# Moving the activation buffers of a four-layer fp32 kernel to other addresses in SBUF, relative to the weight blocks

## The chip, the cores and the metric

One core of a Trainium2 chip. The metric is the device time of one execution in microseconds (us); lower is better. TensorE is called PE in the profile, and its weight loads PEld; DVE is VectorE, ACT is ScalarE, POOL is GpSimd, SP is SyncE.

## The reference, cut to what matters

The kernel computes two fp32 blocks one after the other for 512 tokens of width 1024: a layer with an RWKV-7 mixer, a layer with a convolution mixer (each followed by cross attention to 256 memory tokens and a feed-forward network of width 2816), then a layer with gated linear attention and softmax attention side by side and its own feed-forward network. Nearly all arithmetic is the dense products with weights:

```python
for layer in range(DEPTH):                       # 2
    h = rmsnorm(x, norm_mix_g[layer])
    out = rwkv7_time_mix(h, ...) or conformer_conv(h, ...)
    x = x + out
    x = x + memory_cross_attention(rmsnorm(x, norm_xattn_g[layer]), memn, w_q, w_kv, w_o)
    x = x + conv_ffn(rmsnorm(x, norm_ffn_g[layer]), ffn_w_in[layer], ffn_dw[layer], ffn_w_out[layer])
...
def conv_ffn(h, w_in, dw, w_out):
    u = causal_dwconv(h @ w_in, dw)
    gate, val = u[..., :D_FF], u[..., D_FF:]
    return (jax.nn.silu(gate) * val) @ w_out
```

## The kernel before, in words

Activations are held transposed: 128 partitions times (8 feature tiles, 512 tokens). The weights come from HBM as 388 units of 8 blocks; a block is 128x128 fp32, which is 512 bytes in each partition. SP loads a unit into one of four slots of `raw`, ACT copies it rounded to the format fp32r into `wh` (L1135), and POOL subtracts the two and writes the rest into `wl` (L489). Activations are split in the same way into a high and a low part: `acth` and `actl`, `hidh` and `hidl`, `headh` and `headl`, `memh` and `meml`, `mixh` and `mixl`, `yh` and `yl`. The helper `product` (L504) multiplies one block: three products (high by high, low by high, high by low), each in two halves of 256 tokens, so six matmuls of 256 columns, and each of them loads its weight block into PE by a weight load of its own. A dense stage is a loop over units: 48 matmuls for each output tile of 128 features (8 blocks), 132 for the second product of the feed-forward networks (22 blocks). The order on every engine is fixed by the program text and by semaphores; no scheduler moves anything.

The line in `product` that the text speaks of:

```python
for w, m, first, last in ((w_h, hi, start, False), (w_h, lo, False, False), (w_l, hi, False, stop)):
    for n in range(0, out.shape[1], HALF):
        ins = pe.matmul(out[:, n:n + HALF], w, m[:, n:n + HALF], ...)
```

SBUF is laid out by hand. `place` puts a buffer at the cursor, rounds its size up to 32 bytes and moves the cursor on; `at` puts one at a given address. The cursor starts at byte 2048 of each partition. First come the buffers that live all the time (`raw`, `wh`, `wl`, the residual stream `xt`, `acth`, `actl`, the parameters `par`, the constants `common`, the small vector `omu`, `tmp`, `sq`, `rstd`), then the zone (`zone` is its first byte), which every stage lays out anew: the buffers `mix*`, `head*`, `mem*`, `hid*` and `y*`, and those of the attention and scan stages, lie there. All steps within a buffer by which a matmul's operand is chosen in a dense stage (block, slot, feature tile, half of the tokens) are multiples of 512 bytes, so where an activation buffer lies relative to the weights modulo 512 is one number for each buffer, and every matmul of `product` from it has the same.

Worked out from the sizes: `wh` lies at 18432 and `wl` at 34816, both whole numbers of 512 from each other. `xt` has 8 x 513 columns, 16416 bytes, and ends at 67616, which is 32 bytes beyond a whole number of blocks from the weights. `acth` begins there and `actl` 16384 later. The zone begins at 115904, 192 bytes beyond a whole number.

Of the kernel before, what the change touches and what calls it, by code (L numbers as in the profile page):

```python
# [27 lines left out]
P = 128  # L28
D = 1024
KT = D // P  # L30
# [49 lines left out]
NPAR = _c  # L80
# [88 lines left out]
def build_program(nc, dram):  # L169
# [55 lines left out]
    with ctx:  # L225
        cursor = [2048]

        def size(shape):
            return 4 * int(np.prod(shape[1:]))

        def at(name, shape, dtype, offset):
            assert offset + size(shape) <= nc.sbuf_usable_end, (name, offset)
            return nc.alloc_sbuf_tensor_at(name, shape, dtype, offset=offset)

        def place(name, shape, dtype=F32):
            t = at(name, shape, dtype, cursor[0])
            cursor[0] += (size(shape) + 31) // 32 * 32
            return t
# [2 lines left out]
            return ctx.enter_context(nc.semaphore(name))  # L241


        raw = place("raw", [P, SLOTS, BLOCKS * P])
        wh = place("wh", [P, SLOTS, BLOCKS * P], F32R)
        wl = place("wl", [P, SLOTS, BLOCKS * P], F32R)
        xt_at = cursor[0]
        xt = place("xt", [P, KT, T + 1])
        act_at = cursor[0]
        acth = place("acth", [P, KT, T], F32R)  # L250
        actl = place("actl", [P, KT, T], F32R)
        par = place("par", [P, NPAR])
        common = place("common", [P, 3 * P])
        omu = place("omu", [P, 7 * KT])
        eps = place("eps", [P, 6])
        tmp_at = cursor[0]
        tmp = place("tmp", [P, 2, T])
        sq_at = cursor[0]
        sq = place("sq", [P, 2, T])
        rstd_at = cursor[0]  # L260
        rstd = place("rstd", [P, T])
        zone = cursor[0]
        ident, ones, blk64 = (common[:, j * P:(j + 1) * P] for j in range(3))
        b_eps, b_ln, b_gn, b_rn, b_q, b_eps2 = (eps[:, j:j + 1] for j in range(6))
# [40 lines left out]
        def both(name, shape, n):  # L305

            return [[core(f"{name}{g}{j}", shape) for j in range(n)] for g in range(2)]

        c_core = place("c_core", [P, 7, CH])
        m_n16, m_a, m_be, ident64 = c_core[:, 0, :], c_core[:, 1:4, :], c_core[:, 4:6, :], c_core[:, 6, :]  # L310
        ND, T1, CC = (both(n, [P, 4, CH], 2) for n in ("nd", "t1", "cc"))
        AN, BE, VB = (both(n, [P, m, 4, CH], 2) for n, m in (("an", 3), ("be", 2), ("vb", 2)))
# [2313 lines left out]
```

## Time and profile before

| | |
|---|---|
| median of 3 runs | 2825.18 us (2824.49, 2825.18, 2836.0) |
| the profiled execution | 2821.63 us |
| its span (first to last instruction) | 2819.8 us |
| PE busy | 2632.6 us, 93% of the span, 26234 matmuls |
| PE weight loads busy | 2470.4 us, 88% |
| DVE, ACT, POOL busy | 1451.2, 1158.7, 947.3 us |
| mean granted TensorE clock | 0.965 of full speed |

The profile comes from one execution, and its rows are read against that execution's own 2821.63 us. Matmuls overlap one another in the pipeline, so the mean duration of one (some 280 ns) is longer than the distance between the starts of two; the pace is read from a count in a stretch of time.

### The profile page before, as it was taken

The page shows a single profiled execution, that of the slowest core. Times are in us where ns is not written, and L with a number is a line of the kernel's source. Part 1 is how long each engine was busy: PE and PEld are TensorE (multiplying, and loading weights), DVE is VectorE, ACT ScalarE, POOL GpSimd, SP SyncE. Part 2 cuts the span into 40 slices and gives each one's busy share as a digit, 9 for nine tenths or more (in the row PEclk, how much of TensorE's full clock was granted, in tenths as well). Part 3 has the DMA queues.
Part 4 walks back from the last instruction along what each step waited for, and adds up shares of the span by engine and source line. Part 5 has one row for each costly group of instructions (what it writes and reads, how often), then busy time and mean ns, then how long its engine had stood idle before and what let it go on. Part 6 is the DMA issues. An engine that isn't in the chain of part 4 may idle for free.

```text
span 2819.8 us, 64649 instructions
## 1 busy us (share of the span) xinstructions
PE 2632.6 (93%) x26234; PEld 2470.4 (88%) x26234; DVE 1451.2 (51%) x2006; ACT 1158.7 (41%) x1666; POOL 947.3 (34%) x392
## 2 busy tenths in 40 slices
PE   4897899888999999999899999999999889999997
PEld 4885899687799999978697999999998758999997
DVE  6567544341267775289653677743143234655521
ACT  6542333435354443332543444334246532544432
POOL 1332000025234444433441344444443202444442
PEclk6998899989999999999899999999999999999999
DMA  2221000114122223322321222233222101222231
GB/s 106 75 86 57 4 5 5 65 54 156 60 69 92 100 90 105 104 98 74 106 83 38 90 89 97 98 105 117 85 91 72 42 5 53 98 89 90 100 103 65
DMA packets 61126, 219.92 MB, mean 78 GB/s; under 512 B 6688, under 2 KB 7072, under 8 KB 60320
## 3 DMA queue, kind: packets, MB, share of 16 engines
q1 hardware_dynamic: 57536, 206.43, 21.6%
q10 hardware_dynamic: 3424, 11.01, 1.0%
q8 instruction: 137, 2.24, 0.3%
q14 instruction: 29, 0.24, 0.0%
HBM read 213.22 MB, written 4.19 MB: 77 GB/s over the span
## 4 chain that ended last, share of the span: by engine, by line
PE 66%; issue 21%; DVE 8%; ACT 3%; POOL 3%; DVEq 0%; POOLq 0%; ACTq 0%
PE psum L504 59%; DVE psum L2229 5%; POOL wl L489 3%; PE psum L870 1%; PE psum L827 1%; PE psum L1045 1%; PE psum L1044 1%; DVE tmp L1837 0%; ACT wh L1135 0%; DVE fox_max L2422 0%; PE psum L1067 0%; PE psum L858 0%; DVE fox_p L2447 0%; PE psum L1047 0%; PE psum L547 0%
## 5 line engine op out<-in xcount | busy, mean ns | idle before, releaser
L489 POOL TENSOR_TENSOR wl<-raw,wh 128x1024 fp32r<-128x1024 f32 x388 | 947.1, 2446 | 1839.9 <-ACT wh L1135 1838.7
L504 PE MATMUL psum<-acth,wh 128*128 128x256 f32 x3808 | 769.8, 284 | 34.9 <-DVE actl L1794 18.1
L504 PE MATMUL psum<-actl,wh 128*128 128x256 f32 x3808 | 759.1, 281 | 0.0
L504 PE MATMUL psum<-acth,wl 128*128 128x256 f32 x3808 | 758.8, 281 | 0.0
L504 PEld LDWEIGHTS psum<-acth,wh 128*128 128x128 f32 x3808 | 587.8, 190 | 55.2 <-issue 30.8
L1135 ACT ACTIVATE wh<-raw 128x1024 fp32r<-128x1024 f32 x388 | 407.2, 1056 | 527.9 <-PE psum L504 527.4
L504 PEld LDWEIGHTS psum<-actl,wh 128*128 128x128 f32 x3808 | 587.3, 190 | 0.0
L504 PEld LDWEIGHTS psum<-acth,wl 128*128 128x128 f32 x3808 | 586.9, 190 | 0.0
L2159 DVE TENSOR_TENSOR cu<-psum,rstd 128x512 f32<-128x512 f32 x132 | 91.0, 690 | 235.1 <-PE psum L504 220.4
L504 PE MATMUL psum<-hidl,wh 128*128 128x256 f32 x1056 | 205.6, 276 | 0.0
L504 PE MATMUL psum<-hidh,wl 128*128 128x256 f32 x1056 | 205.6, 276 | 0.0
L504 PE MATMUL psum<-hidh,wh 128*128 128x256 f32 x1056 | 205.5, 276 | 0.0
L1833 DVE TENSOR_TENSOR xt<-xt,delta 128x512 f32 x56 | 40.4, 721 | 245.3 <-ACT delta L1220 245.1
L504 PEld LDWEIGHTS psum<-hidl,wh 128*128 128x128 f32 x1056 | 159.0, 188 | 0.0
L504 PEld LDWEIGHTS psum<-hidh,wl 128*128 128x128 f32 x1056 | 158.9, 188 | 0.0
L504 PEld LDWEIGHTS psum<-hidh,wh 128*128 128x128 f32 x1056 | 158.9, 188 | 0.0
L2229 DVE SCALAR_TENSOR_TENSOR psum<-gp,par,psum 128x512 f32<-128x512 f32 x210 | 142.3, 751 | 1.6
L1837 DVE TENSOR_SCALAR tmp<-xt,par 128x512 f32 x48 | 124.3, 2590 | 12.0 <-DVE xt L1833 12.0
L1518 ACT ACTIVATE ffn_sg<-ffn_cg 128x512 f32<-128x512 f32 x66 | 41.8, 634 | 145.4 <-DVE ffn_cg L2182 112.9
L504 PE MATMUL psum<-memh,wh 128*128 128x256 f32 x256 | 74.7, 292 | 7.1 <-POOL wl L489 7.1
L2176 DVE SCALAR_TENSOR_TENSOR ffn_cg<-cu,par,ffn_cg 128x512 f32<-128x512 f32 x44 | 79.8, 1814 | 0.0
L504 PE MATMUL psum<-headh,wh 128*128 128x256 f32 x384 | 76.9, 282 | 0.0
(409 smaller groups left out, 3985.0 us busy)
## 6 DMA issues: line engine op xcount, KB each, us to landing
raw<-in_weights SPq DMA_DIRECT2D x388, 512.0 KB, 3.4
xt<-in_x SPq DMA_DIRECT2D x4, 512.0 KB, 5.6
xt<-in_x ACTq DMA_DIRECT2D x1, 2048.0 KB, 9.3
out_x<-xt ACTq DMA_DIRECT2D x4, 512.0 KB, 2.9
mem<-in_mem ACTq DMA_DIRECT2D x1, 1024.0 KB, 11.1
memn<-memh ACTq DMA_DIRECT2D x1, 1024.0 KB, 3.9
memn<-meml ACTq DMA_DIRECT2D x1, 1024.0 KB, 6.8
memh<-memn ACTq DMA_DIRECT2D x1, 1024.0 KB, 7.0
```

What stands on the lines that cost most here:

```text
L489: pool.tensor_tensor(wl[:, s, :], raw[:, s, :], wh[:, s, :].bitcast(F32), ALU.subtract).then_inc(split_done, 1)
L504: ins = pe.matmul(out[:, n:n + HALF], w, m[:, n:n + HALF], start=first and n == 0, stop=last and n + HALF >= out.shape[1])
L827: ins = pe.matmul(bank[4 + tt // 2][:, (tt % 2) * MEM:(tt % 2 + 1) * MEM], query[:, 2 * h + k, tt * P:(tt + 1) * P], keys[:, 2 * h + k, :] ...
L870: ins = pe.matmul(bank[t % 4][:, :], vtok[:, mt, (2 * h + dt) * P:(2 * h + dt + 1) * P], probt[:, h % 2, mt, :], start=(mt == 0), stop=(mt ...
L1044: pe.matmul(bank[b][:, o:o + n], fq[r, p, qt * P:n], fk[r, p, 0:n], start=True, stop=False)
L1135: act.activation(wh[:, s, :], raw[:, s, :], ACT.Identity).then_inc(split_hi, 1)
L1518: act.activation(sg[:, s, :], cg[:, s, :], ACT.Silu if l < 2 else ACT.Gelu_apprx_tanh).then_inc(gate_ready, 1)
L1833: dve.tensor_tensor(xk, xk, buf[:, s, :], add).then_inc(x_ready, 1)
L1837: dve.tensor_scalar(t_, xk, pc(gain[0], k + col), pc(gain[1], k) if n == 2 else None, mul, mul if n == 2 else ALU.bypass).then_inc(val_rea ...
L2159: dve.tensor_tensor(cu[:, s, 2:T + 2], bank_of(t0 + s), rstd[:, :], mul).then_inc(evacuated, 1)
L2176: chain.step(dve.scalar_tensor_tensor(out=to, in0=cu[:, s, 1:T + 1], scalar=pc("ffn_dw", col + 1), in1=to, op0=mul, op1=add))
L2229: ins = dve.scalar_tensor_tensor(out=acc, in0=gp[:, k, j:j + T], scalar=pc("conv_dw", k * CONVW + j), in1=acc, op0=mul, op1=add)
```

## The change

A helper moves the cursor on to the next address that lies a given number of bytes beyond a whole number of 512 from the weights. It is called with 0 ahead of `acth` and with 64 ahead of the zone. `par`, `common` and `eps` now stand ahead of `acth`, and the vector `omu` (one minus the mixing factors, 224 bytes, used in the first mixer) is put into the first stage's zone, at its end.

```diff
+        def beside_weights(apart):
+            cursor[0] += (weights_at + apart - cursor[0]) % 512
+
         raw = place("raw", [P, SLOTS, BLOCKS * P])
+        weights_at = cursor[0]
         wh = place("wh", [P, SLOTS, BLOCKS * P], F32R)
         wl = place("wl", [P, SLOTS, BLOCKS * P], F32R)
         xt_at = cursor[0]
         xt = place("xt", [P, KT, T + 1])
+        par = place("par", [P, NPAR])
+        common = place("common", [P, 3 * P])
+        eps = place("eps", [P, 6])
+        beside_weights(0)
         act_at = cursor[0]
         acth = place("acth", [P, KT, T], F32R)
         actl = place("actl", [P, KT, T], F32R)
-        par = place("par", [P, NPAR])
-        common = place("common", [P, 3 * P])
-        omu = place("omu", [P, 7 * KT])
-        eps = place("eps", [P, 6])
         tmp_at = cursor[0]
         tmp = place("tmp", [P, 2, T])
         sq_at = cursor[0]
         sq = place("sq", [P, 2, T])
         rstd_at = cursor[0]
         rstd = place("rstd", [P, T])
+        beside_weights(64)
         zone = cursor[0]
...
         c_core = place("c_core", [P, 7, CH])
+        omu = place("omu", [P, 7 * KT])
```

Worked out from the sizes, the addresses and what they leave modulo 512 from the weights:

```
buffer                                     before            after
wh, wl, raw, xt                            0                 0
acth, actl                                 67616, 84000: 32  72704, 89088: 0
tmp, sq, rstd (midh, midl lie in sq)       192               0
zone: mix, head, mem, hid, y, gmid, ...    115904: 192       115776: 64
par / common                               32 / 448          32 / 448
```

No instruction is added, taken away or moved: on each of the five engines the list of instructions with their operands and shapes reads the same before and after, and only line numbers and addresses differ.

## Rows read from the trace of the kernel before

**Rows 1.** The page's first parts: busy time, and the span in 40 slices.

```profile
PE 2632.6 (93%) x26234; PEld 2470.4 (88%) x26234; DVE 1451.2 (51%) x2006; ACT 1158.7 (41%) x1666; POOL 947.3 (34%) x392
PE   4897899888999999999899999999999889999997
...
PEclk6998899989999999999899999999999999999999
```

**Rows 2.** The page's chain that ended last, by engine and by line.

```profile
PE 66%; issue 21%; DVE 8%; ACT 3%; POOL 3%; DVEq 0%; POOLq 0%; ACTq 0%
PE psum L504 59%; DVE psum L2229 5%; POOL wl L489 3%; PE psum L870 1%; PE psum L827 1%; PE psum L1045 1%; PE psum L1044 1%; DVE tmp L1837 0%; ACT wh L1135 0%; DVE fox_max L2422 0%; PE psum L1067 0%; PE psum L858 0%; DVE fox_p L2447 0%; PE psum L1047 0%; PE psum L547 0%
```

**Rows 3.** Groups by line and shape, PE: count, busy us, mean ns, idle before.

```profile
L504 PE MATMUL psum<-acth,wh 128*128 128x256 f32 x3808 | 769.8, 284 | 34.9 <-DVE actl L1794 18.1 <-DVE actl L1845 6.6 <-DVE actl L2299 5.5
...
L504 PE MATMUL psum<-hidh,wh 128*128 128x256 f32 x1056 | 205.5, 276 | 0.0
L504 PE MATMUL psum<-headh,wh 128*128 128x256 f32 x384 | 76.9, 282 | 0.0
...
L504 PE MATMUL psum<-memh,wh 128*128 128x256 f32 x256 | 74.7, 292 | 7.1 <-POOL wl L489 7.1
...
L504 PE MATMUL psum<-mixh,wh 128*128 128x256 f32 x176 | 40.2, 314 | 20.0 <-DVE mixl L1794 20.0
...
L504 PE MATMUL psum<-yh,wh 128*128 128x256 f32 x128 | 24.9, 276 | 0.0
```

**Rows 4.** Windows, PE: stretch, length, busy us (matmuls), granted clock, DMA.

```profile
880.00:1060.00 180.00, 180.00 (x1545) 1.00 0.28 94
1080.00:1190.00 110.00, 110.00 (x974) 1.00 0.31 106
```

**Rows 5.** The chain in order of time: start us, us, what; the PE pieces.

```profile
696.07 22.41 PE psum L504 x192
...
721.93 22.63 PE psum L504 x192
...
783.00 43.55 PE psum L504 x384
834.54 360.50 PE psum L504 x3120
1256.28 15.90 DVE psum L2229 x24
...
1459.04 22.61 PE psum L504 x192
1485.11 16.97 PE psum L504 x144
1540.64 43.55 PE psum L504 x384
1592.19 360.50 PE psum L504 x3120
1961.67 67.22 PE psum L504 x576
...
2442.39 360.52 PE psum L504 x3120
```

**Rows 6.** The timeline at 44 us, PE, granted clock at half: start, us.

```profile
44.20 0.63 PE L504 MATMUL psum<-mixh,wh 128*128 128x256 f32 x2
44.63 0.63 PE L504 MATMUL psum<-mixl,wh 128*128 128x256 f32 x2
```

**Rows 7.** The timeline from 2177.5 us, weight loads (PEld): start, us.

```profile
2177.56 0.98 PEld L992 LDWEIGHTS psum<-sct,gvt 128*128 128x128 f32 x8
2178.66 1.30 PEld L995 LDWEIGHTS psum<-gqk,gla_states 64*128 64x128 f32 x11
```

**Rows 8.** Windows, all engines, the convolution stage: busy us of each.

```profile
1195.00:1375.00 180.00, 164.28 (x1148) 140.06 (x1146) 164.32 (x241) 62.03 (x101) 69.88 (x29) 0.97 0.30 100
```

## The prediction

> **What bounds the kernel now.** I read the page first. PE is busy 93% of the span and its clock is granted in full in nearly all slices after the start [rows 1]; the chain that ended last is made of PE for 66%, and 59% of the span is the one line of `product` [rows 2]. "issue" in that chain is mostly the scan of small matmuls and the start, which the change does not touch. So the pace at which PE starts the matmuls of `product` sets most of the time, and the next question is whether this pace depends on where an operand lies. The groups by line and shape answer it in part: the mean durations differ by operand, 284 ns for `acth` and 276 for `hidh` and `yh`, though shape and weights are alike [rows 3]. Durations are not paces, so I take counts in windows. From 880 to 1060 us PE does nothing but the first product of a feed-forward network, from `acth` and `actl`: 1545 matmuls touch the 180 us, and as each lasts 0.28 us the pace is (180 + 0.28) / 1545 = 116.7 ns. From 1080 to 1190 us it is the second product, from `hidh` and `hidl`: (110 + 0.28) / 974 = 113.2 ns. The clock is 1.00 in both [rows 4]. The chain confirms it: 834.54 us begins a piece of 360.50 us with 3120 matmuls, which are 2064 from `act` (43 tiles of 48) and 1056 from `hid`; 2064 x 116.7 = 240.9, and what is left gives 119.6 / 1056 = 113.3 ns [rows 5]. It does not come from other engines: windows with POOL, ACT and DMA working in the same way show both paces, and each buffer keeps its own for over a thousand matmuls.
>
> Shorter pieces of the chain show the rest [rows 5]. Buffer `act`: 22.41 / 192 = 116.7, 67.22 / 576 = 116.7, but 22.63 / 192 = 117.9. Zone buffer `head`: 43.55 / 384 = 113.4 twice, but 22.61 / 192 and 16.97 / 144 = 117.8. So the buffers 32 bytes beyond a whole number of blocks run at 116.7 or 117.9, those 192 beyond at 113.3 or, rarely, at 117.8; a stream keeps the pace with which it set out.
>
> **How far down the pace could go.** 256 columns at 2.4 GHz are 106.7 ns; 113.3 and 116.7 are 6.6 and 10.0 above. At the half clock there is nothing above: two matmuls in 0.43 us, 215 ns each as the rounded starts give it, against 256 / 1.2 GHz = 213.3 [rows 6]. The loss exists only where both streams of PE (moving columns, weights) read at full speed, which fits reads that meet in SBUF. The weight loads have a floor of their own: in L995 each has only 64 columns to wait for, and the loads still start (1.30 - 0.19) / 10 = 111 ns apart; in L992 (0.98 - 0.19) / 7 = 113, of which the first distance is the longest [rows 7]. I take 111.7 as the floor of a load of 128 columns, since `product` has one load for each matmul. The changed pace lies between that and something above 117.9.
>
> **The change part by part.** No instruction is added, removed or moved, so all that can change is a duration.
>
> `acth`, `actl` from 32 to 0. Three groups of 3808, 11424 matmuls [rows 3]. Bounds from the rows: 111.7 below, and above 117.9 plus what closeness may add (below). I take 113.3, the pace of the buffers that lie an even number of 64 bytes from the weights, because the difference between 113.3 and 116.7 is 3.4 ns, which is 8 columns or 32 bytes of the moving stream at full clock: just what a start 32 bytes off a 64-byte line would add, and 0 has none of that. Certain to count are the 3 x 2064 = 6192 of the three long pieces, where the chain is PE alone [rows 5]: 6192 x 3.4 = 21.1 us. Of the other 5232, 768 stand in the convolution stage, where DVE is busy 164.3 of 180 us and the chain goes through its taps (15.90 us of L2229) [rows 5, 8]: they count nothing. The remaining 4464 run at 116.7 or 117.9, half and half, so 4.0 ns each, 17.9 us; some stand beside waits of PE on DVE and ACT (34.9 us before `acth`) [rows 3] or at the half clock, and I count 80%: 14.3 us.
>
> The zone from 192 to 64. 3 x (1056 + 384 + 256 + 176 + 128) = 6000 matmuls [rows 3], at 113.3 nearly all. 64 is again a whole number of 64-byte lines, so by the same reading nothing changes, except that the 336 matmuls of `head` at 117.8 may fall to 113.4: 336 x 4.4 = 1.5 us. Bounds: 111.7 gives 1.6 x 6000 x 0.9 = 8.7 us more, 116.7 (the pace of 32, the nearest value seen) costs 3.4 x 6000 x 0.9 = 18 us.
>
> `tmp`, `sq`, `rstd`, `par`, `common`, `omu`. DVE, ACT and POOL read and write them, and no row ties a duration of theirs to an address. `omu` is used only in the first mixer. Nothing, and if it were something, it would be hidden behind PE at 93%.
>
> What keeps pace: ACT and POOL have to split a unit per tile, 48 x 113.3 = 5.4 us, and POOL needs 2.4 us for one (947.3 us for 388); DMA is at 0.28. None becomes the bound; DVE between the tiles of a long piece does not either, since PE waits for it 0.0 us before `hidh` [rows 1, 3, 4].
>
> Sum: 21.1 + 14.3 + 1.5 = 37 us off the profiled execution's 2821.6, 2785. The median of the runs stands 3.6 us above the profiled one, so 2788.
>
> By the Trainium skill, "SBUF — State Buffer", section on who interferes with whom, the two read ports of PE are independent and PE never waits on anyone. If so, addresses could not matter and the sum would be 0; the rows show 113.3 against 116.7 at the same clock and shape, so on this point the trace does not agree. Its page "TensorE: Matmul & The Clock Gate", section on the back-to-back gap, gives N / 2.4 + 2.5 ns, 109.2 for 256 columns. No row of `product` gets there; by it the estimate would be some 95 us less, about 2730, and I give it no more than 0.03, within the second case below.
>
> **The rivals.**
>
> Both buffers at the floor of the loads, 111.7. For: a start at the same line lets the two streams meet where the load pauses between blocks; the fp32 products L992, whose operands `sct` and `gvt` lie a whole number of 512 apart, show loads at the same distance as L995 [rows 7]. Against: no buffer of `product` shows it now. Price: 6192 x 5.0 + 4464 x 5.6 x 0.8 + 8.7 + 1.5 = 61 us; 2764.
>
> `act` gains, the zone loses. 64 is nearer to 32 than to 192. Then -35 + 18 = -17; 2809.
>
> Nothing. The pace is set by how a stream starts, not by the address: `head` is seen at 113.4 and at 117.8 at one address [rows 5], and the sums of both kinds stay as they are. Against: no `act` piece is below 116.7 and all three long `hid` pieces are at 113.3. 2825.
>
> Slower. What costs is closeness: when the moving stream and the weights begin in the same part of SBUF, they meet at once and stay together. 192 costs 6.6 and 32 costs 10.0 ns, 0.7 more for 32 bytes less; continued, 0 gives 117.4 and 64 gives 116.0: 0.7 x 10000 + 2.7 x 5400 = +22 us, 2847. L992 speaks against it, but its 128 columns fill 112 ns, so that stream reads half as fast and can yield. It decides as soon as the zone goes above 113.3 by more than `act` comes down: at a zone of 116.7 (+18 us) `act` would have to gain less than 1.8 ns on its 10000.
>
> **How the numbers follow.** `act` at 113.3 with the zone as it is: 0.38. Both near the floor, or between: 0.24. `act` gains and the zone loses: 0.12. Nothing: 0.10. Slower: 0.16. The likeliest gives 2788. About 0.5%, 14 us, is what a measurement of this kernel can tell from no change. Faster by more holds the first two cases and most of the third, 0.72; within it 0.11; slower 0.17. The range runs from 2757, a little below the floor case, to 2832, which leaves out the slower case and little else.
>
> **What would show it.** In the profile after: the window of the first product of a feed-forward network with (180 + 0.28) / 0.1133 = 1591 matmuls in 180 us instead of 1545, each of the three long pieces at 3120 x 0.1133 = 353.5 us instead of 360.5, the mean of `acth` near 276 as `hidh` has now, and `hidh` unchanged. At 1614 in 180 us, or 348.5 us, it is the floor of the loads. 1545 or fewer is the end of this reading; so is a `hid` pace above 113.3, which would say that 64 is worse than 192. The prediction is wrong if the 117.8 pace, whose start I cannot read from any row, becomes the usual one at the new addresses, or if other waits of PE take up the time that the long pieces give back.

## The result, and the profile after

The change made the kernel slower: 2869.52 us median of 4 runs (2860.37 to 2879.96) against 2824.84 us of 4 (2822.17 to 2836.0), a ratio of 1.0152 with a 95% interval of 1.0106 to 1.0198. The prediction was 2788 us, in a range of 2757 to 2832, and gave slower 0.17. The profile comes from the shortest of the four executions.

The page of the changed kernel (lines are 7 further down: `product` is L511) answers to [rows 1, 2]:

```profile
span 2858.6 us, 64649 instructions
...
PE 2672.1 (93%) x26234; PEld 2516.0 (88%) x26234; DVE 1435.0 (50%) x2006; ACT 1157.6 (40%) x1666; POOL 945.9 (33%) x392
...
PE psum L511 64%; PE psum L648 8%; DVE psum L2236 5%; PE psum L834 1%; PE psum L877 1%; PE psum L1052 1%; PE psum L1051 1%; POOL wl L496 1%; PE psum L576 1%; DVE tmp L1844 0%; ACT wh L1142 0%; DVE fox_max L2429 0%; DMA c_post<-in_c_post 0%; PE psum L1074 0%; DVE prep_pt L1955 0%
```

PE is busy 39.5 us longer (2672.1 against 2632.6), DVE, ACT and POOL are not, and the span is 38.8 us longer. That points to PE's own pace. The shares of the chain do not say it: L648, the small matmuls of the scan, has 8% here and did not show before, and "issue" fell from 21% to 6%, though the stretch that holds the scan (from the end of `mix` to the next products of `act`) took 433.8 us against 431.8; the chain was followed through it another way. Two windows of the changed kernel answer to [rows 4]; the second begins 10 us later, since the second product itself begins 9 us later:

```profile
880.00:1060.00 180.00, 180.00 (x1502) 1.00 0.26 90
1090.00:1200.00 110.00, 110.00 (x936) 1.00 0.30 103
```

With the last digits as in the prediction: (180 + 0.28) / 1502 = 120.0 ns for `acth` and `actl` at distance 0 (bytes beyond a whole number of 512 from the weights), where 32 had 116.7; (110 + 0.28) / 936 = 117.8 ns for `hidh` and `hidl` at 64, where 192 had 113.2. The clock is 1.00 in both, as before. The chain in order of time has the same pieces as [rows 5], each longer:

```profile
698.70 23.04 PE psum L511 x192
...
725.19 23.04 PE psum L511 x192
...
783.43 45.24 PE psum L511 x384
...
836.67 372.06 PE psum L511 x3120
...
1606.51 372.06 PE psum L511 x3120
1987.58 69.11 PE psum L511 x576
...
2469.96 372.06 PE psum L511 x3120
```

Every piece of `act` now gives one pace, 23.04 / 192 = 69.11 / 576 = 120.0, and `head` 45.24 / 384 = 117.8 where it had 113.4. The three long pieces are 372.06 - 360.50 = 11.56 us longer each, 34.7 of the 38.8 us in all.

### The profile page after: what moved, and what is told of

The parts are those of the page before. It is cut to its first block, busy times and chain, and to the rows that moved or that the text cites. A ratio compares the mean times of both kernels' runs of the same rounds, so it can differ in the third digit from the quotient of the medians.

```text
span 2858.6 us, 64649 instructions
## 1 busy us (share of the span) xinstructions
PE 2672.1 (93%) x26234; PEld 2516.0 (88%) x26234; DVE 1435.0 (50%) x2006; ACT 1157.6 (40%) x1666; POOL 945.9 (33%) x392
## 4 chain that ended last, share of the span: by engine, by line
PE 79%; DVE 10%; issue 6%; ACT 3%; POOL 1%; DMA 0%; DVEq 0%; ACTq 0%; POOLq 0%
PE psum L511 64%; PE psum L648 8%; DVE psum L2236 5%; PE psum L834 1%; PE psum L877 1%; PE psum L1052 1%; PE psum L1051 1%; POOL wl L496 1%; PE psum L576 1%; DVE tmp L1844 0%; ACT wh L1142 0%; DVE fox_max L2429 0%; DMA c_post<-in_c_post 0%; PE psum L1074 0%; DVE prep_pt L1955 0%
## 5 line engine op out<-in xcount | busy, mean ns | idle before, releaser
L511 PE MATMUL psum<-acth,wh 128*128 128x256 f32 x3808 | 781.9, 287 | 37.3 <-DVE actl L1801 21.1
L511 PE MATMUL psum<-actl,wh 128*128 128x256 f32 x3808 | 771.0, 284 | 0.0
L511 PE MATMUL psum<-acth,wl 128*128 128x256 f32 x3808 | 770.6, 284 | 0.0
L511 PEld LDWEIGHTS psum<-acth,wh 128*128 128x128 f32 x3808 | 598.7, 193 | 57.9 <-issue 30.6
L511 PEld LDWEIGHTS psum<-actl,wh 128*128 128x128 f32 x3808 | 598.1, 193 | 0.0
L511 PEld LDWEIGHTS psum<-acth,wl 128*128 128x128 f32 x3808 | 597.5, 193 | 0.0
L511 PE MATMUL psum<-hidl,wh 128*128 128x256 f32 x1056 | 210.3, 280 | 0.0
L511 PE MATMUL psum<-hidh,wh 128*128 128x256 f32 x1056 | 209.4, 280 | 0.0
L511 PE MATMUL psum<-hidh,wl 128*128 128x256 f32 x1056 | 209.3, 279 | 0.0
L511 PEld LDWEIGHTS psum<-hidh,wl 128*128 128x128 f32 x1056 | 161.3, 188 | 0.0
L511 PEld LDWEIGHTS psum<-hidh,wh 128*128 128x128 f32 x1056 | 161.2, 187 | 0.0
L511 PEld LDWEIGHTS psum<-hidl,wh 128*128 128x128 f32 x1056 | 161.2, 188 | 0.0
L511 PE MATMUL psum<-memh,wh 128*128 128x256 f32 x256 | 74.7, 292 | 7.2 <-ACT keys L1451 7.2
L511 PE MATMUL psum<-headh,wh 128*128 128x256 f32 x384 | 77.9, 283 | 0.0
```

The source lines that it names most:

```text
L511: ins = pe.matmul(out[:, n:n + HALF], w, m[:, n:n + HALF], start=first and n == 0, stop=last and n + HALF >= out.shape[1])
```

## The experiments

The question was what sets a pace. My reading had been the start on a 64-byte line; the result pointed to the distance of the two operands, but one number for each of two buffers, in one kernel, does not show that, and the second pace of `head` before was unexplained. Theory A is that the distance modulo some period decides; the rivals are the other engines, the start on a line, the place of the moving buffer by itself, and the stream that ran before.

### The pace by itself, for 16 distances (e1_pace)

```diff
+seen = [at(f"d{d:03d}x", [P, 4, T], F32R, 67584 + 18432 * (i % 2) + d) for i, d in enumerate(OFFSETS)]
...
+for k in range(8):
+    for j, s in enumerate((0, 0, 1)):
+        for h in range(0, T, HALF):
+            ins = pe.matmul(bank[w % 4][:, h:h + HALF], weights[:, s, k * P:(k + 1) * P],
+                            m[:, k % 4, h:h + HALF], ...)
```

> This kernel leaves the whole computation out except a stream of matmuls like product's, and copies x to the output. For each of 16 distances (0, 32, ... 480 bytes, modulo 512) between the moving buffer and the weights it runs six stretches of 48 fp32r matmuls of 256 columns, each stretch begun after a wait on VectorE of another length, and two stretches of 24 matmuls of 512 columns. No DMA runs, and ScalarE and VectorE do next to nothing. Theory A (the distance modulo 512 alone sets the pace, by the two read streams of TensorE meeting in SBUF): about 120.0 ns at 0, 116.7 at 32, 117.8 at 64, 113.3 at 192, as in the kernels before and after, with nothing else running. Theory B (reads and writes of the other engines make the loss): with them silent every distance goes at one pace, 109 to 113 ns. Theory C (what my prediction took: a start off a 64-byte line is what costs): the odd multiples of 32 are 3.4 ns slower than the even ones everywhere, which the 120 ns at 0 in the changed kernel already speaks against. For 512 columns with one load each the load is no limit: 213.3 ns plus at most 10, so at least 5 ns less for each 512 columns than two of 256.

The timeline of this kernel, PE: start us, us, and the idle time ahead. L243 is a stretch of 48 matmuls of 256 columns, L237 one of 24 with 512; the number in the name is the distance in bytes.

```profile
27.87 6.01 PE L243 MATMUL psum<-d000x,weights 128*128 128x256 f32 x48 [0.76 <-DVE step L219]
...
62.35 5.75 PE L237 MATMUL psum<-d000x,weights 128*128 128x512 f32 x24 [0.97 <-DVE step L219]
...
136.40 5.92 PE L243 MATMUL psum<-d064x,weights 128*128 128x256 f32 x48 [0.76 <-DVE step L219]
...
170.41 5.79 PE L237 MATMUL psum<-d064x,weights 128*128 128x512 f32 x24 [0.97 <-DVE step L219]
...
353.73 5.73 PE L243 MATMUL psum<-d192x,weights 128*128 128x256 f32 x48 [0.76 <-DVE step L219]
...
380.07 5.92 PE L243 MATMUL psum<-d192x,weights 128*128 128x256 f32 x48 [0.92 <-DVE step L219]
386.96 5.86 PE L237 MATMUL psum<-d192x,weights 128*128 128x512 f32 x24 [0.97 <-DVE step L219]
...
461.59 6.02 PE L243 MATMUL psum<-d256x,weights 128*128 128x256 f32 x48 [0.76 <-DVE step L219]
```

In such a stretch the first two starts are 0.22 us apart and the last matmul lasts 0.28 us, so 6.01 is (6.01 - 0.22 - 0.28) / 46 = 119.8 ns, 5.92 is 117.8, and 5.73 is 113.7, of which the first few starts are up to 124 ns apart and all later ones 113.3. From the starts of all stretches, once they are steady, in ns:

```
distance   0     32           64     96     128            160          192                 224
256 col.   120.0 116.7, 117.8 117.8  120.0  118.6          117.4, 118.7 113.3 x5, 117.8 x1  118.3
distance   256   288          320    352    384            416          448                 480
256 col.   120.0 116.7, 117.8 117.8  120.0  118.6, 120.0   117.4, 118.8 113.3 x5, 117.8 x1  118.3
512 col.: 226.7 at 0 and 256; 228.9 at 64 and 320; 233.2 to 234.5 at all others
```

Nothing else runs beside these stretches but, at most distances, four copies by ScalarE of 0.6 us each, and the paces of both kernels come back to the tenth of a ns: theory B is out. The period is 256 bytes, not 512, as far as steps of 32 bytes can tell. Theory C, mine, is out too: 0 and 96 are both the slowest, 64 and 128 are no better than 160. And for one distance there can be two paces; after its first few starts a stretch keeps to one of them.

### One part of the change at a time, and both buffers at 192 (e2_act_only, e3_zone_only, e4_both_192)

```diff
-        beside_weights(0)          # e2: 0      e3: 32     e4: 192
+        beside_weights(A)
...
-        beside_weights(64)         # e2: 192    e3: 64     e4: 192
+        beside_weights(Z)
```

> The changed kernel with the zone back at 192 and acth, actl at 0. Theory A: the first product of each feed-forward network at 120.0 ns (1502 matmuls in 180 us), the second at 113.3; of the 39 us between the two spans the act part, some 24 us, stays: about +0.9% on the kernel before. Theory B2 (the zone or the moved small buffers carry the loss): no different from before.

> The changed kernel with acth, actl back at 32 and the zone at 64. Theory A: the first product at 116.7, the second at 117.8; the zone's part of 3 x 1056 x 4.4 = 14 us and some 6 us of head, y and mix stay: +0.7% on the kernel before. Theory B2 (acth carries all): no different from before.

> Both acth, actl and the zone at 192, with the order of buffers of the changed kernel. Theory A: both products at 113.3 ns, every long piece of 3120 matmuls 353.5 us instead of 360.5, in all some 30 us less than before, -1.1%. Rival (the pace is that of the buffer and stage, or of who writes it, and not of the distance): acth stays at 116.7 or above and the time is that of before.

Ratios to the kernel before, run again beside them (19 executions, median 2827.0 us), with intervals: e2 1.0074 (1.0055 to 1.0093), e3 1.0020 (1.0006 to 1.0033), e4 1.0050 (1.0028 to 1.0072). The chain's first long piece and the two windows of each:

```profile
832.57 367.38 PE psum L511 x3120
...
880.00:1060.00 180.00, 180.00 (x1502) 1.00 0.27 90
1090.00:1190.00 100.00, 100.00 (x885) 1.00 0.32 105
```

is e2: `act` at 120.0, `hid` at (100 + 0.28) / 885 = 113.3, as theory A said, and its +0.74% near the +0.9%. e3, and below it e4:

```profile
845.37 360.50 PE psum L511 x3120
...
880.00:1060.00 180.00, 180.00 (x1546) 1.00 0.28 95
1090.00:1200.00 110.00, 110.00 (x973) 1.00 0.31 106
```

```profile
699.15 21.79 PE psum L511 x192
...
724.39 22.63 PE psum L511 x192
...
838.82 367.48 PE psum L511 x3120
...
880.00:1060.00 180.00, 180.00 (x1531) 1.00 0.27 93
1090.00:1200.00 110.00, 110.00 (x937) 1.00 0.30 101
```

Both missed. In e3 `hid` lies at 64, where the changed kernel had 117.8, and runs at (110 + 0.28) / 973 = 113.3, in all three long pieces; `head`, `mix` and `y` did go to 117.8 as foretold, which is the part of the loss that stayed. In e4 `act` and `hid` lie at 192, and all three long pieces run at 117.8, while a shorter piece of the same `act` in the same execution, 21.79 / 192 = 113.5 at 699.15 us, has the fast pace and the next one, 22.63 us, again the slow one. So both paces belong to one buffer at one address, and the distance alone does not say which comes. The times agree with this: e4 went from 2824.8 to 2852.9 us over 10 runs, and its two executions at a granted clock of 0.963 were 2824.8 and 2852.8 us, so the clock does not make that difference. The spread by itself would be a weak sign: the kernel before stayed within 2821.9 and 2833.2 over these 19 executions, but within 2812.4 and 2834.1 over the 17 beside e5 to e7.

### What the stream before does (e8_entry)

```diff
+                    stream(lead[i], 8, 0)
+                    ins = stream(m, 16, 1)
```

> This kernel leaves the whole computation out except streams of matmuls of 256 columns like product's. For each pair of distances (from 0, 32, 64, 192 to 0, 32, 64, 192) it runs, four times after waits of different length, 48 matmuls at the first distance and then, with no pause, 96 at the second. Theory D (two paces are possible at 64 and at 192, 113.3 and 117.8 ns, and the stream that runs just before decides which one is taken up; once taken up it stays): at 192 the pace is 113.3 after 0 and after the 116.7 pace of 32, and 117.8 after a stream at 117.8; at 64 it is 117.8 after 0 and 113.3 after 32; at 0 it is 120.0 after anything. Theory E (the distance alone decides, and the 113.3 of the hid buffers at 64 in the run with the zone alone moved had another cause): 64 is at 117.8 after every lead.

The timeline, 96 matmuls each, begun with no pause behind a stream at the distance named first:

```profile
641.31 11.47 PE L228 MATMUL psum<-from000to064x,weights 128*128 128x256 f32 x96
...
695.49 11.05 PE L228 MATMUL psum<-from032to064x,weights 128*128 128x256 f32 x96
...
712.99 11.47 PE L228 MATMUL psum<-from032to064x,weights 128*128 128x256 f32 x96
...
998.60 11.05 PE L228 MATMUL psum<-from032to192x,weights 128*128 128x256 f32 x96
...
1051.29 11.05 PE L228 MATMUL psum<-from064to192x,weights 128*128 128x256 f32 x96
...
1068.86 11.47 PE L228 MATMUL psum<-from064to192x,weights 128*128 128x256 f32 x96
```

11.47 is (11.47 - 0.28) / 95 = 117.8 ns and 11.05 is 113.4. At 0 all 16 streams go at 120.0. At 192, all eight behind a lead at 0 or 32 take 113.3. Behind a lead at 192 itself each stream keeps its lead's pace, 113.3 three times and 117.8 once. Behind a lead at 64, which ran at 117.8 all four times, two take 117.8 and two 113.3. At 64, 117.8 comes in 15 of 16, and 113.3 once, behind 32. That fits theory D at 0, and at 192 but for the two of four behind 64; and it fits the two cases of the kernels: `hid` at 64 behind `act` at 0 is at 117.8 (the changed kernel), behind `act` at 32 it can be at 113.3 (e3). It is not a rule one can plan with: three of four streams behind 32 went to 117.8, though theory D had said 113.3; and the pace of the lead does not settle it, for of the two whose lead ran at 116.7 one took 113.3 and one 117.8. At 32 I had written nothing down, and there the lead shows most clearly: 117.8 in all four behind 0, 116.7 in all four behind 192, the lead's own pace behind 32, and behind 64 twice 116.7 and twice 120.0, a third pace.

### One matmul of 512 columns for two of 256 (e5_wide_0_0, e6_wide_after, e7_wide_before)

```diff
-                    for n in range(0, out.shape[1], HALF):
-                        ins = pe.matmul(out[:, n:n + HALF], w, m[:, n:n + HALF], start=first and n == 0,
-                                        stop=last and n + HALF >= out.shape[1])
+                    ins = pe.matmul(out, w, m, start=first, stop=last)
```

e5 has `beside_weights(0)` for the zone too, e6 the changed kernel's addresses, e7 those of before.

> The changed kernel with the zone at 0 as well as acth, actl, and product with one matmul of 512 columns (one weight load) in place of two of 256. From the stretches of 512 columns in the pace kernel (226.7 ns at 0): 113.35 ns for each 256 columns in every dense stage of 512 tokens, and no second pace. Against before: 3.4 ns on some 10000 matmuls of 256 columns less, 1.5 us of head; the memory stages stay at 256 columns and go to 120.0, +5 us. In all -33 us, -1.2%. Rival (512 columns lose it again elsewhere: longer first and last matmuls, PSUM banks freed later): between -0.5% and 0.

> The changed kernel (0 and 64) with matmuls of 512 columns. acth, actl at 113.35 per 256 columns, the zone at 228.7 / 2 = 114.35: -28 us against before, -1.0%, and some 70 us less than the changed kernel with halves. If the addresses of the change are bad in themselves, it stays slower than before.

> The kernel before (32 and 192) with matmuls of 512 columns: 233.3 / 2 = 116.7 for both, so acth as it was and the zone 3.3 ns slower: +15 us, +0.5%. If fewer weight loads were a gain by themselves, whatever the distance, it would be faster by the same 1% as the other two.

Measured against the kernel before, run again beside them (17 executions): e5 0.9878 (0.9854 to 0.9903), 2788.6 us against 2824.8; e6 0.9892 (0.9864 to 0.9920); e7 1.0045 (1.0028 to 1.0061). All three are within 0.1% of where the pace kernel put them, and the first long piece of each chain, in this order, is what it should be, 1560 x 226.7 = 353.6 us for e5:

```profile
833.17 353.63 PE psum L510 x1560
```

```profile
832.05 354.82 PE psum L510 x1560
```

```profile
836.51 364.01 PE psum L503 x1560
```

So the addresses of the change are bad for matmuls of 256 columns and good for those of 512, as the two rows of the table have it. At the old addresses fewer weight loads gain nothing: e7 has them there and is slower than before. e5 is faster than both kernels and its runs lie within 2783.6 and 2792.8.

### Is it the length of the weight load (e9_narrow)?

```diff
+                                elif w < 8:
+                                    ins = pe.matmul(out[0:64, :], weights[:, s, k * P:k * P + 64], m[:, k % 4, h:h + HALF], start=first, stop=last)
+                                else:
+                                    ins = pe.matmul(out[0:32, :], weights[:, s, k * P:k * P + 32], m[:, k % 4, h:h + HALF], start=first, stop=last)
```

> This kernel leaves the whole computation out except streams of matmuls of 256 columns. At 8 distances (0, 32, ... 224) it runs four stretches of 48 with weight loads of 128 columns, four with loads of 64 and four with loads of 32, the moving side unchanged. Theory A2 (the loss above 109 ns is what the weight load's read and the moving read cost each other in SBUF): with a shorter load the streams overlap for less time, so the loss shrinks, to about a half at 64 columns (some 113 to 115 ns at 0) and a quarter at 32, and the differences between distances shrink with it. Theory F (the loss belongs to the moving read alone, to where it starts): the paces at each distance stay as they are with 128 columns.

The timeline, stretches of 48; L239 loads 128 weight columns, L241 64, L243 32:

```profile
28.29 6.01 PE L239 MATMUL psum<-d000x,weights 128*128 128x256 f32 x48 [0.76 <-DVE step L219]
...
48.86 5.67 PE L241 MATMUL psum<-d000x,weights 128*64 128x256 f32 x48 [0.88 <-DVE step L219]
...
75.49 5.84 PE L243 MATMUL psum<-d000x,weights 128*32 128x256 f32 x48 [1.05 <-DVE step L219]
...
109.66 5.87 PE L239 MATMUL psum<-d032x,weights 128*128 128x256 f32 x48 [0.76 <-DVE step L219]
...
129.79 5.92 PE L241 MATMUL psum<-d032x,weights 128*64 128x256 f32 x48 [0.88 <-DVE step L219]
```

Both theories failed. At 0 the paces are 120.0, 113.3 and 117.8 for loads of 128, 64 and 32 columns; at 32 a load of 64 is slower, 119.0, than one of 128, 116.7. So the load takes part, which rules out theory F, but the loss does not shrink with its length. Over the eight distances each of the three lengths has paces from 113.3 to 120.0, only at other distances (loads of 32 columns reach 113.3 at 64, 128, 160 and 192), and no stretch of any width is below 113.3.

### Distance, or the place of the moving buffer (e10_grid)

```diff
+        ws = {s: at(f"w{s:03d}x", [P, 2, 4 * P], F32R, 18432 + 4352 * i + s) for i, s in enumerate(shifts)}
+        seen = [at(f"m{d:03d}x", [P, 2, T], F32R, 67584 + 4608 * n + d) for n, (s, d) in enumerate(OFFSETS)]
```

> This kernel leaves the whole computation out except streams of matmuls of 256 columns. The weights lie at four places (0, 32, 64, 192 bytes beyond a multiple of 256) and the moving buffers at four, all 16 pairs, six stretches of 48 each. Theory A (the distance counts): the pace depends on moving minus weights modulo 256: every pair at equal places at 120.0 ns, moving 192 beyond the weights (weights 64 and moving 0; weights 0 and moving 192) at 113.3 for most starts, moving 64 beyond the weights (192 and 0, 0 and 64) at 117.8, moving 224 beyond (64 and 32, 32 and 0) at 118.3, moving 128 beyond (64 and 192) at 118.6. Theory G (the absolute place of the moving buffer counts, since the weights have never moved in any run so far): each moving place keeps its pace whatever the weights' place, 120.0 at 0, 117.8 at 64, 113.3 at 192, and the change would do the same without any weights near.

The groups by line and shape, PE: count, busy us, mean ns. Six stretches of 48 each, so less busy time is a faster pace:

```profile
L227 PE MATMUL psum<-m032x,w032x 128*128 128x256 f32 x288 | 36.1, 285 | 4.9 <-DVE step L219 4.9
L227 PE MATMUL psum<-m192x,w192x 128*128 128x256 f32 x288 | 36.1, 285 | 4.9 <-DVE step L219 4.9
L227 PE MATMUL psum<-m064x,w064x 128*128 128x256 f32 x288 | 36.1, 285 | 4.9 <-DVE step L219 4.9
...
L227 PE MATMUL psum<-m192x,w000x 128*128 128x256 f32 x288 | 34.9, 281 | 4.9 <-DVE step L219 4.9
L227 PE MATMUL psum<-m000x,w064x 128*128 128x256 f32 x288 | 34.5, 279 | 4.9 <-DVE step L219 4.9
```

All four pairs at equal places are at 120.0 in every steady stretch, wherever that place is; a moving buffer at 0 runs at 120.0 with the weights at 0, 118.3 with them at 32, 113.3 (five of six) at 64, and 117.8 (five of six) at 192. The paces at each difference modulo 256 are those of e1_pace, but for one stretch of six at 113.3 in each of the two pairs with 64, and 117.8 in three of six, not one, for weights at 0 and moving at 192; which of two paces comes stays open here too. The same holds for the two differences that had no place in the expectation: 160 (moving 192, weights 32) at 117.4 and 118.7, and 96 (moving 32, weights 192) at 120.0. Theory G is out. Each of these small kernels was run once, on four different chips, and their paces agree.

## Why the prediction was wrong, point by point

- **What bounds the kernel** was right: the pace of `product`, which differs by buffer at one clock, and which other engines do not make [e1_pace]. The three long pieces carry 34.7 of the 38.8 us by which the profiled span grew.
- **The step that failed** is the one that put `act` at 0 at 113.3: "the difference between 113.3 and 116.7 is 3.4 ns ... just what a start 32 bytes off a 64-byte line would add". Two distances had been seen, 32 and 192, and I made a rule of them by one coincidence of size; no row showed a 64-byte line, and no run does. 0 runs at 120.0, and so does 96, and 128 at 118.6 [e1_pace]. In place of the rule stands a table with a period of 256 bytes that rises and falls: 0 is among the worst of its entries and 192 the best. So the term of the long pieces, 21.1 us off, became 6192 x 3.3 = some 20.5 us on.
- **The zone at 64, "by the same reading nothing changes"**, failed with it: 117.8 in 3168 matmuls of `hid` and all of `head` and `y`, where nearly all had 113.3; `hid` alone is 3168 x 4.5 = some 14 us on. Only `mem` had one of its two stages at 113.3 in the changed kernel. The bound of +3.4 ns for the zone was too low by 1.1.
- **The slower rival** ended on the right side and had the wrong mechanism. Closeness, continued from 192 to 32 to 0, gave 117.4 and 116.0 against 120.0 and 117.8, hence 2847 for 2869.5. It falls as a rule too: 96 is farther than 32 and slower, 224 is no better than 64. L992 had "spoken against it"; its operands lie a whole number of 256 apart, but it is plain fp32 with 128 columns, and what holds for it says nothing of 256 columns of fp32r.
- **The rival "nothing"**, by which the pace hangs on how a stream starts, was partly right: two paces exist at 32, 64, 192 and other distances, and the stream before can decide between them [e8_entry]. But at 0 only one was ever seen, and that is where the change put two thirds of the matmuls of `product`.
- **The rule of the Trainium skill**, from "SBUF — State Buffer", section on who interferes with whom, that PE's two read ports are independent, had been set aside against the rows. The runs keep it aside: with every other engine idle, moving either operand by 64 bytes changes the pace by up to 6.7 ns [e10_grid].
- **The 80% for the pieces beside waits** can't be judged by this profile. Outside the long pieces some 4464 matmuls of `act` became 2.2 or 3.3 ns slower and some 2000 of the zone about 4.4, some 22 us together, and the span shows 4.1 us of it. But the two profiled executions had unlike clocks, 0.965 before and 0.976 after as the mean, which is (1 - 0.965) x 2 x 2819.8 = 197 us at half clock against 137. Two neighbouring stretches, the same work before and after (start and end, length, PE busy, clock, DMA), before first:

```profile
1961.63:2057.46 95.83, 95.05 (x807) 1.00 0.26 91
2057.46:2345.57 288.11, 260.83 (x1671) 0.95 0.14 46
```

```profile
1987.53:2085.88 98.35, 97.56 (x806) 1.00 0.26 88
2085.88:2370.60 284.72, 257.99 (x1671) 0.98 0.14 47
```

  Where both have the full clock the slower pace comes through whole, 98.35 - 95.83 = 2.52 us for 766 matmuls of `act` at 3.3 ns; where the clock is better after, the stretch is 3.4 us shorter in spite of it. Of the four executions of the changed kernel the profiled one, 2860.4 us, had the highest clock; the one at 0.965, the clock of the profile before, took 2880.0. So the 38.8 us between the profiles are probably too little (the medians lie 44.7 us apart), and how much the waits absorbed stays open.
- **A reading of the prediction** was off in a small term: "116.7 or 117.9, half and half". In the trace of the kernel before, some 1100 matmuls of `act` outside the long pieces ran at 117.8 and some 3800 at 116.7, so the mean gain would have been 3.6 ns and not 4.0, and the term 13 us and not 14.3. The rest of the sum adds up as written.

Two limits of the mechanism stay open. The runs show that the loss depends on the difference of the two addresses modulo 256; they do not show what in SBUF or in PE makes it, nor whether a stream without a load for each matmul would have it, which no run tried, and the guess that it is the two reads overlapping failed in e9_narrow as a matter of duration. And what decides between two paces at one distance after a wait was not found; only that a stream, once steady, keeps its pace until there is a pause or another buffer's turn.

## What to carry to other kernels

When matmuls of one shape from two buffers have different paces at one clock, sweep the address difference between moving buffer and weights in a small kernel with nothing else in it before placing anything: 16 distances took one execution of 0.9 ms, and its table then foretold three full kernels with 512 columns to 0.1%. For 256 columns, where a distance can have two paces, no full kernel was foretold from it, and of those built on the distance alone two of three missed. Two points of such a function are no rule, and one buffer's best distance changes with the number of columns: place for the shape that runs. Prefer a distance with one pace to one with a faster and a slower one, unless the stream before it is under control.

## What the runs showed of the hardware that I had not expected

- The pace of fp32r matmuls of 256 columns with a load each depends on moving minus weight address modulo 256 bytes: 120.0 ns at 0 and 96, 113.3 at best at 192 (117.8 in other stretches), at the full 2.4 GHz. At the half clock (1.2 GHz) the starts were 213 to 214 ns apart whatever the buffer: `mix` at 192 and `act` at 32 in the kernel before, `mix` at 64 and `act` at 0 in the changed one.
- For 512 columns the order is another: 226.7 ns at 0, 228.9 at 64, 233.2 to 234.5 elsewhere [e1_pace].
- At one distance there can be two stable paces, 113.3 and 117.8, which last for thousands of matmuls: with both buffers at 192, what had been the best distance, 3120 of them took 367.48 us at 117.8, and 192 from the same `act` took 21.79 us at 113.5 [e4_both_192].
- A shorter weight load can make the matmul slower: at 32, 119.0 ns with 64 columns against 116.7 with 128 [e9_narrow].
